# Modulation vectors of a diffusion backbone: the conditioning held in four column groups of the tensor array, its rows turned and added in three pieces, and six weight slots in place of four

## The reference

```python
for l in range(DEPTH):
    mod_l = (jax.nn.silu(c) @ ada_w[l] + ada_b[l])[:, None, :]
    mod_c = jax.nn.silu(c_ctx) @ ada_w[l] + ada_b[l]
    sh1, sc1, g1, sh2, sc2, g2 = jnp.split(mod_l, N_MOD, axis=-1)
    ...
    a_lat = modulate(rmsnorm(h_lat, norm1_g[l]), sh1, sc1)
    ...
    h_lat = h_lat + g1 * y_lat
    h_lat = h_lat + g2 * peer_ffn(modulate(rmsnorm(h_lat, norm2_g[l]), sh2, sc2), ...)
```

## Time and profile before

| | us |
|---|---|
| median of 3 runs | 3653.57 |
| lowest and highest run | 3648.0, 3656.35 |
| the profiled execution | 3648.24 |
| its span in the trace | 3646.4 |

### The profile page before, as it was taken

How to read it: one execution, slowest core, us unless ns; L and a number is a source line. 1 busy time by engine, 2 the same in 40 slices (tenths; PEclk the granted TensorE clock), 3 DMA queues, 4 the chain that set the end, 5 groups by cost and what they waited for, 6 DMA issues and landing times.

```text
span 3646.4 us, 47438 instructions
## 1 busy us (share of the span) xinstructions
PE 3426.9 (94%) x19384; PEld 2917.3 (80%) x19384; DVE 1979.2 (54%) x3330; ACT 1191.8 (33%) x1795; POOL 20.0 (1%) x41
## 2 busy tenths in 40 slices
PE   8899897999999999999999999798468999999998
PEld 7465546888888888888888888688458999999998
DVE  2204633488855555634444444333935998856665
ACT  1111224322233333333333333424314444444443
POOL 0000000000000000000000000000000000000000
PEclk9889898999999999999999999899789999999999
DMA  5241012355555556576556655222014777788885
GB/s 175 70 128 46 1 41 95 114 168 162 166 166 199 193 182 203 173 246 201 192 190 193 193 190 161 69 83 91 0 58 157 211 212 243 246 275 265 266 260 168
DMA packets 232862, 587.87 MB, mean 161 GB/s; under 512 B 21239, under 2 KB 104264, under 8 KB 229000
## 3 DMA queue, kind: packets, MB, share of 16 engines
q1 hardware_dynamic: 227536, 528.57, 46.2%
q0 software_dynamic: 4208, 53.27, 3.8%
q10 hardware_dynamic: 904, 3.01, 0.2%
HBM read 483.06 MB, written 101.71 MB: 160 GB/s over the span
## 4 chain that ended last, share of the span: by engine, by line
PE 87%; DVE 10%; ACT 2%; issue 1%; DMA 1%; ACTq 0%; SPq 0%; DVEq 0%
PE ps L501 42%; PE ps L743 30%; PE ps L657 7%; PE ps L699 5%; DVE w_lo L1459 1%; PE ps L556 1%; DVE arena L1376 1%; PE ps L618 1%; PE ps L679 1%; DVE arena L1370 1%; PE ps L807 0%; PE ps L626 0%; ACT a_t L890 0%; DVE arena L1611 0%; DVE arena L1378 0%
## 5 line engine op out<-in xcount | busy, mean ns | idle before, releaser
L1459 DVE TENSOR_TENSOR w_lo<-wring,w_hi 128x1024 fp32r<-128x1024 f32 x512 | 626.0, 1223 | 736.5 <-ACT w_hi L1008 735.0
L501 PE MATMUL ps<-a_hi,w_hi 128*128 128x512 f32 (+1 forms) x2048 | 703.6, 344 | 8.5 <-DVE w_lo L1459 4.4
L743 PE MATMUL ps<-act_hi,w_hi 128*128 128x512 f32 (+1 forms) x2048 | 697.6, 341 | 3.4 <-DVE act_lo L1490 3.4
L501 PE MATMUL ps<-a_hi,w_lo 128*128 128x512 f32 (+1 forms) x2048 | 690.5, 337 | 0.0
L501 PE MATMUL ps<-a_lo_q,w_hi 128*128 128x512 f32 (+1 forms) x2048 | 690.0, 337 | 0.0
L743 PE MATMUL ps<-act_lo,w_hi 128*128 128x512 f32 (+1 forms) x2048 | 688.8, 336 | 0.0
L743 PE MATMUL ps<-act_hi,w_lo 128*128 128x512 f32 (+1 forms) x2048 | 688.3, 336 | 0.0
L1008 ACT CAST w_hi<-wring 128x1024 fp32r<-128x1024 f32 x512 | 534.3, 1044 | 226.3 <-PE ps L743 226.2
L501 PEld LDWEIGHTS ps<-a_hi,w_hi 128*128 128x128 f32 x2048 | 390.0, 190 | 48.6 <-DVE w_lo L1459 7.0
L743 PEld LDWEIGHTS ps<-act_hi,w_hi 128*128 128x128 f32 x2048 | 388.5, 190 | 50.1 <-issue 3.6
L501 PEld LDWEIGHTS ps<-a_hi,w_lo 128*128 128x128 f32 x2048 | 389.6, 190 | 42.0
(11 more groups left out here) (226 smaller groups left out, 3597.4 us busy)
## 6 DMA issues: line engine op xcount, KB each, us to landing
wring<-in_u SPq DMA_DIRECT2D x256, 512.0 KB, 4.1
wring<-in_v SPq DMA_DIRECT2D x256, 512.0 KB, 4.1
gates<-arena POOLq DMA_DIRECT2D x24, 2048.0 KB, 7.6
acts<-arena SPq DMA_DIRECT2D x128, 256.0 KB, 4.6
arena<-acts SPq DMA_DIRECT2D x128, 256.0 KB, 3.5
arena<-gates SPq DMA_DIRECT2D x16, 2048.0 KB, 11.4
aring<-in_ada SPq DMA_DIRECT2D x56, 512.0 KB, 5.1
wring<-in_ada SPq DMA_DIRECT2D x40, 512.0 KB, 3.7
```

The source lines that it names most:

```text
L501: ins = pe.matmul(o, l, r, start=n == 0, stop=n == len(pairs) - 1, **kw)
L743: ins = pe.matmul(value_sum(l, c), w, x, start=m == 0 and n == 0 and (l == 0 or c % 2 == 0), stop=m == NKEY - 1 and n == 2, skip_group_che ...
L1459: tt(WLO[:, k % 4].rearrange("p k n -> p (k n)"), wring[:, n % RING * TILE:(n % RING + 1) * TILE], WHI[:, k % 4].rearrange("p k n -> p (k ...
```

## The change

- **Operands swapped.** The conditioning is now stationary, padded from 2 to 32 columns with zeros (`cpad`, CP), and the weights move: two tiles, 256 columns, in one matmul. The matmul of block k writes to partitions 32·(k mod 4) and up, so that the eight blocks go to four groups of 32 array columns, two blocks to each. A group g is now always two tiles and eight matmuls (`rows`): 48 groups in all, 8 at the start, 12 in the input product, 28 late.
- **Turned.** The result has outputs along the free dimension and lies in four partial sums. ACT copies its 128x256 to SBUF (`rows_in`, into `arows`, the upper half of `hand`), and PE turns it and adds the four with two matmuls of 128x2 against a selector (`turned`, `rowsel`), into bank 4. `rowsel` is made on DVE from the identity.
- **Three additions.** DVE adds the bias to the 16 tiles of the start, the 24 of the input product and the 56 late ones in one instruction each. `hyena` on PE waits for the second, since `hand` is used again there.
- **Late passes** stand in every second turn from 56 to 110, two tiles each, loaded by one DMA to two buffers over the space of the routing (`LATE_W`); `aring` is gone. SP waits for the last routing (`gates_ready`) ahead of these loads.
- **Ring of six.** RING is 6, in the space that `aring` had. Two tiles of a group must lie side by side in it, so that in even passes j of the input product the group stands ahead of the pass (`ada_leads`). SP's loops are written out.

`ada` in the last piece of the diff is on DVE and is called three times; `rows_in` is on ACT, the rest on PE.

```diff
-RING = 4
+RING = 6
+def ada_leads(j):
+    return j < AB_GROUPS and (AT_ABIN + 3 * j + 1) % RING == RING - 1
-LATE_TURN = {2 * j + 1: j for j in range(ADA_LATE)}
+LATE_TURN = {FIRST_OCT + 2 + 2 * j: j for j in range(LATE_GROUPS)}
...
+            def rows(g, w, done):
+                bank = 5 + g % 2 if g < EARLY_GROUPS else 5
+                wait(pe, S["rows_in"], g - 1 if g < EARLY_GROUPS else g)
+                for k in range(KD):
+                    q = 32 * (k % 4)
+                    ins = pe.matmul(ps[q:q + 32, bank, 0:256], CP[:, k, :], w[:, :, k, :], start=k < 4, stop=k >= 4)
+                ins.then_inc(S[done], 2)
...
-                for j in range(count):
-                    n = pos + j
-                    landed(pe, n)
-                    group(ps[:, 5 + g % 2, 2 * j:2 * j + 2],
-                          [(W[:, n % RING, k, :], CS[:, k, :]) for k in range(KD)], "w_used")
+                for x in range(2):
+                    landed(pe, ADA_AT[g] + x)
+                r = ADA_AT[g] % RING
+                rows(g, W[:, r:r + 2], "w_used")
...
+            def turned(g):
+                if g == 0:
+                    pe.wait_ge(S["sel_ready"], 1)
+                pe.wait_ge(S["rows_in"], g + 1)
+                for x in range(2):
+                    m = 2 * g + x
+                    ins = pe.matmul(ps[:, 4, 2 * m:2 * m + 2], arows[:, m % 4 * P:(m % 4 + 1) * P],
+                                    rowsel[:, :], start=True, stop=True)
+                ins.then_inc(S["rows_turned"], 1)
...
+            def rows_in(g):
+                if g < EARLY_GROUPS:
+                    act.wait_ge(S["w_used"], ADA_AT[g] + 2)
+                else:
+                    act.wait_ge(S["late_used"], 2 * (g - EARLY_GROUPS + 1))
+                wait(act, S["rows_turned"], g - 1)
+                bank = 5 + g % 2 if g < EARLY_GROUPS else 5
+                copy(arows[:, 256 * (g % 2):256 * (g % 2) + 256], ps[:, bank, 0:256]).then_inc(S["rows_in"], 1)
...
+            def ada(g0, g1):
+                m0, m1 = 2 * g0, 2 * g1
+                dve.wait_ge(S["rows_turned"], g1)
+                tt(M2[:, m0:m1, :], ps[:, 4, 2 * m0:2 * m1].rearrange("p (m z) -> p m z", z=2),
+                   adab[:, m0:m1].unsqueeze(2).to_broadcast([P, m1 - m0, 2]), ALU.add).then_inc(S["ada_taken"], 1)
```

More of the change, by code:

```diff
@@ L367, in _, with load @@
             sp.dma_start(csil[:, :], a["cc"]).then_inc(S["c_in"], 16)
[L369 to L371 removed]
+            def load(n, src):
+                wait(sp, S["w_used"], n - RING + 1)
                 sp.dma_start(wring[:, n % RING * TILE:(n % RING + 1) * TILE], src).then_inc(w_loaded[n % RING], 16)
[L374 to L375 removed]
@@ L398, in late, with stream, stream_abin, ab @@
-            def late(j):
-                wait(sp, S["late_used"], j - 1)
-                sp.dma_start(aring[:, j % 2 * TILE:(j % 2 + 1) * TILE], a["ada"][LATE_AT + j])\
-                    .then_inc(S[f"late_loaded{j % 2}"], 16)
+            def stream(n0, src, count):
+                for j in range(count):
+                    load(n0 + j, src[j])
+            def stream_abin():
+                def ab(j):
+                    load(at_abin(j), a["abin"][j])
+                for j in range(N_ABIN):
+                    if not ada_leads(j):
+                        ab(j)
+                    if j < AB_GROUPS:
+                        for x in range(2):
+                            load(at_ada_ab(j) + x, a["ada"][ADA_FIRST + ADA_AB * j + x])
+                    if ada_leads(j):
+                        ab(j)
@@ L420, in first_products @@
                     load(n0 + k, u[k])
[L421 removed]
+                for m in range(NKEY + ZRING):
                     if m < NKEY:
@@ L828, in _ @@
             ada(0)
-            ada(1)
+            for g in range(3):
+                ada(g + 1)
+                turned(g)
             filters()
@@ L872, in filters @@
                     act.activation(FHID[n], FARG, ACT.Sin).then_inc(S["f_sin"], 1)
+                    for g in range(4 + 2 * n, 6 + 2 * n):
+                        rows_in(g)
                 for t in range(2):
@@ L916, in ab_in @@
                     copy(dst, ps[:, j % 4, :]).then_inc(S["ab_taken"], 1)
+                    if j < AB_GROUPS and not ada_leads(j):
+                        rows_in(FIRST_GROUPS + j)
                     c = j - 1
@@ L1123, in _ @@
             act.activation(lbs[:, 32:64], lbs[:, 32:64], ACT.Exp).then_inc(S["lb_exp"], 1)
+            for g in range(4):
+                rows_in(g)
             filters()
```

118 lines of the change are left out of this document (65 added, 53 removed).

## The result

The changed kernel takes 3531.49 us (median of 4, 3529.78 to 3535.15) against 3654.96 us (3648.0 to 3657.0) for the kernel before: a ratio of 0.9667, 95% interval 0.965 to 0.9684. That is 123 us less; the forecast of the likeliest case was 57 to 61 less. The rival in which all four column groups overlap had 3530 us.

A forecast was written before the change was run, and what follows sets the result against it. PE was taken to bound the kernel. Late groups -26, input product -20 and start -11 sum to -57 us: 3591 from the profiled run, 3596.6 from the median, given as 3594; 8-in-10 range 3526 to 3660.

The forecast's parts named there:

- the likeliest case: Whole kernel: a pass of 1.95 us, 2.73 us a group at full clock, 57 us saved; 3570 to 3612 us, chance 0.52.
- The rival of full overlap: All modulation passes: four column groups side by side, 0.87 us a pass, 1.65 a group; -121 us, 3530 us; chance 0.16.
- the three places named: Where modulation is computed: start -11 us, input product -20, late groups in layer 0's first products -26.
- point (2): Profile sign, turns 0 to 51: w_lo steps of 5.45 us each; larger means DVE holds PE.
- the wide range: Whole kernel, 8 in 10: 3526 us, taking in full overlap, to 3660, taking in the mildest slower cases.
- the signs of being wrong: A PE wait for `rows_in` or a growing landing wait at the start, a pass near 3.5 us, or gain elsewhere.
- the middle value: Pass of a group: 9 steps, 1.95 us at full clock; only neighbouring records in different column groups overlap.
- the 8 us kept for the clock: Input product: allowance for five new light stretches cooling the clock, 0 if none does, 15.5 us if each does.
- The 18.5 us: Input product: clock loss of the old form, 3.1 us for each of six w_in passes, forecast to go.
- the rival without overlap: All passes: 3.47 us a pass, 4.25 a group, slower by 35 to 58 us, 3695 us; chance 0.18.
- point from which it decides: All three places: the pass may grow by 1.0 us, to 2.97, before the gain is gone.
- Ring of six, "0": Tile ring: 0 us, as PE had no landing wait to lose, except that it keeps the start fed.

The follow-up runs named there:

- Experiments 1 and 5: Matmul issue order changed: 1, changed kernel, 0, 4, 1, 5, 2, 6, 3, 7, 3530.08 us; 5, two-column-group kernel, 0, 2, 4, 6, 1, 3, 5, 7, 3595.28 us.
- experiment 4: Kernel before, each input-product group's first tile moved to the middle of the w_in pass, second behind it: 3630.42 us, its baseline 3648.67.

## Why the prediction was right and wrong

**Direction and places: right.** The gain stands in the three places named and nowhere else, PE bounds the kernel as before, and DVE did not become late: in turns 1 to 51 w_lo follows at 5.48 us on the mean (single steps 4.4 to 6.4), where point (2) asked for 5.45, and PE is busy for all of layer 0's first products. One step of w_lo, then the window:

```profile
713.73 1.23 DVE L1514 TENSOR_TENSOR w_lo<-wring,w_hi 128x1024 fp32r<-128x1024 f32 x1 [0.48 <-ACT w_hi L1060]
719.16 1.23 DVE L1514 TENSOR_TENSOR w_lo<-wring,w_hi 128x1024 fp32r<-128x1024 f32 x1 [1.11 <-ACT w_hi L1060]
```

```profile
622.75:1485.80 863.05, 863.05 (x4669) 719.72 (x4670) 596.50 (x1159) 284.05 (x430) 8.52 (x16) 1.00 0.61 194
```

**The size: wrong.** The likeliest case was to lie between 3570 and 3612 us; 3531 is the time of a rival that had a chance of 0.16, and the wide range holds the result only because it took that rival in. One of the signs of being wrong that the prediction names did show: PE's waits at the start, 5.02 and 1.19 us.

**The pass: wrong.** "Both records of one matmul use the same 32 array columns and so follow each other" holds: the run with one group shows 16 steps. What failed is the reason given for the middle value, that instructions of one queue start in their order. Experiments 1 and 5 show records of one column group being passed by those of another. So four groups make 4 steps, 0.87 us, not 9 and 1.95. At full clock that is 1.08 us in each of 40 passes, 43 us, and 17 us in the eight of the start, of which the new waits there took some 5 back. With the 8 us kept for the clock (below) this makes up the 62 us between forecast and result.

The Trainium skill (TensorE: Matmul & The Clock Gate, "Part 3") has both the span model, by which a pack costs one matmul and about 4 ns for each further tile, and the sentence that matmuls start in program order. The times agree with the first in the main, 0.87 us for the four steps of a pass with 7 ns between the starts of one batch (13 in experiment 1), and experiments 1 and 5 do not fit the second.

**The rival of full overlap** had the right pass, and its terms were near: late -56 (measured -54.8; a group 1.74 us for 1.65), input product -41 (-42.7; a group 1.51), start -24 (-22.7). Its wait of 4.5 us at the start was put down to ACT's first copy; it is a landing tile, 5.02 us, and the copy is 1.19. So the start's term came out near for another reason than the one given.

**The clock: half right.** The 18.5 us were there to be had, experiment 4 gives 18.3. But I kept 8 of them as a risk because the new stretches might be as long, and the rival without overlap was priced with 3.1 to 7.7 us for each long stretch. Neither happened in stretches of 256-column matmuls, even of 7.7 us.

**No overlap would be slower: wrong.** I priced the case of one group at 3695 us; it ran at 3631, below the kernel before (ratio 0.9951, 0.9934 to 0.9968). Its late term was right to a few us, 28 x 2.58 = 72 us above the four groups. The two others were not: the start ran at the full clock from the fourth pass on, where I had 8.53 us a group at half clock, and the input product kept its clock. The "point from which it decides", a pass of 2.97 us, was therefore too low; even 3.58 us is still a small gain, and it is the clock's.

**Ring of six, "0": wrong.** I looked for waits for landing in the trace of before, found none, and took it that the ring had nothing to give. But the new form makes each stretch ask for tiles faster and frees them by twos. Without the two slots, and with the order that the code takes for four, 22 of the 123 us would be lost. The step that failed is reading a resource's worth from the profile of a kernel that used it more slowly.

## What to carry to other kernels

A product with a very narrow moving side costs a weight load for each block of weights, and long runs of it can cost the clock as well. With the narrow side made stationary in four column groups the wide side streams in a quarter of the time that it takes in one (0.87 us against 3.46), and two tiles cost 1.5 to 1.7 us, turning and changes of shape included, where they cost 3.5 to 3.7 before. The order in which the groups alternate cost nothing here with four records of one group in a row, and did with eight. Whatever makes the consumer faster or lumpier has to be given buffers in the same edit: ask of each ring how fast it will be emptied after, not whether anybody waits on it now.

## What the runs showed of the hardware

- Records in distinct 32-column groups overlap fully for float32: 16 records in 4, 8 and 16 steps of 0.216 us with four, two and one group. Order in the queue did not matter with four records of one group in a row; with eight it did (12 steps instead of 8).
- Stretches of two-column matmuls between w_in passes: with 3.49 us the mean granted clock of the stage was 0.84, with 1.71 us (and half as long stretches of w_in work between them) it was 1.00. With stretches of 256-column ones in 32 array columns it was 1.00 even at 7.7 us.
- At the start PE ran at half clock through all passes in the six profiles with four groups and rose to the full one in the six with two groups or one. Whether it stayed there through f_raw (7.67 us in one profile, 12.2 to 12.6 in five) was not settled by what stands in the program.
- The same instructions between hyena and the first products took 359 to 371 us in different profiles, at mean granted clocks of 0.93 to 0.89.
